# Query stage of a two-layer hybrid decoder step: query latents ahead of key latents, rope copies later, value weights split ahead of the meeting, first sample unit ahead of the first prompt unit

## The reference, cut to what matters

```python
cq = rmsnorm(cq, lw["q_norm_g"])
q = (cq @ lw["w_uq"]).reshape(B, T, MLA_HEADS, QK_NOPE + QK_ROPE)
q_pe = rope(q[..., QK_NOPE:], pos)
q_lat = jnp.einsum("bthn,chn->bthc", q[..., :QK_NOPE], lw["w_uk"])
ckv = rmsnorm(ckv, lw["kv_norm_g"])
kpe = rope(kr[:, :, None, :], pos)[:, :, 0, :]
o_lat = attend(q_lat, q_pe, ckv, kpe)
yb = jnp.einsum("bthc,chv->bthv", o_lat, lw["w_uv"]).reshape(B, T, MLA_HEADS * V_HEAD)
```

## Time and profile before

| | |
|---|---|
| median of 3 runs | 2144.66 us (2136.49 to 2145.21) |
| the profiled execution: its time / its span | 2144.24 us / 2142.4 us |
| PE busy | 2054.8 us, 96% of the span |
| PEld busy | 1898.9 us, 89% |
| DVE, ACT, POOL busy | 1199.2 us (56%), 801.8 us (37%), 402.5 us (19%) |
| matmuls | 17374 |

### The profile page before, as it was taken

One profiled execution on the slowest core, in us unless ns is written; L12 is line 12 of the kernel. 1 busy time (PEld: TensorE's weight loads), 2 busy tenths in 40 slices (PEclk: granted clock), 3 DMA queues, 4 the chain that ended last, 5 costly groups with the idle time before them and its releaser, 6 DMA issues.

```text
span 2142.4 us, 43035 instructions
## 1 busy us (share of the span) xinstructions
PE 2054.8 (96%) x17374; PEld 1898.9 (89%) x17374; DVE 1199.2 (56%) x2036; ACT 801.8 (37%) x1504; POOL 402.5 (19%) x407
## 2 busy tenths in 40 slices
PE   7989999999998999999999899999999999999997
PEld 7976667999998999999988766679999899999997
DVE  4755445333578752666757544453335886436665
ACT  4334335222354321334443333352223544213334
POOL 0025662000052000000350266610001600000012
PEclk9999999999999999999999999999999999999999
DMA  7347996222432232225451399952225232212252
GB/s 254 113 148 279 367 367 252 79 83 83 146 117 89 89 104 66 79 78 184 138 204 59 137 349 370 358 199 86 80 88 163 90 107 81 99 63 87 80 193 72
DMA packets 88849, 325.68 MB, mean 152 GB/s; under 512 B 10576, under 2 KB 15568, under 8 KB 88592
## 3 DMA queue, kind: packets, MB, share of 16 engines
q1 hardware_dynamic: 46512, 169.52, 24.2%
q0 software_dynamic: 37440, 144.98, 18.2%
q10 hardware_dynamic: 4768, 9.37, 1.3%
HBM read 315.52 MB, written 7.26 MB: 151 GB/s over the span
## 4 chain that ended last, share of the span: by engine, by line
PE 85%; DVE 9%; ACT 3%; DMA 1%; issue 1%; DVEq 1%; PEldq 0%; ACTq 0%; SPq 0%; PEld 0%
PE PS L1002 65%; PE PS L1283 6%; PE PS L1254 5%; DVE m_WL L1425 3%; PE PS L1274 2%; PE PS L1265 1%; ACT m_WH L548 1%; DVE m_X L1459 1%; DMA m_WS<-in_w_units 1%; PE PS L1306 1%; PE PS L1033 1%; PE PS L1322 1%; DVE m_XS L1470 1%; PE PS L1313 1%; PE PS L1300 1%
## 5 line engine op out<-in xcount | busy, mean ns | idle before, releaser
L1002 PE MATMUL PS<-m_XS,m_WH 128*128 128x288 f32 x5120 | 922.0, 297 | 33.8 <-DVE m_WL L1425 17.8
L1002 PEld LDWEIGHTS PS<-m_XS,m_WH 128*128 128x128 f32 x5120 | 768.0, 189 | 42.5 <-DVE m_WL L1425 20.6
L1002 PE MATMUL PS<-m_XS,m_WL 128*128 128x288 f32 x2560 | 583.5, 297 | 0.0
L1425 DVE TENSOR_TENSOR m_WL<-m_WS,m_WH 128x1024 fp32r<-128x1024 f32 (+2 forms) x284 | 369.6, 1302 | 226.8 <-ACT m_WH L548 217.9
L548 ACT ACTIVATE m_WH<-m_WS 128x1024 fp32r<-128x1024 f32 (+2 forms) x284 | 315.6, 1113 | 372.4 <-PE PS L1002 341.7
L1002 PEld LDWEIGHTS PS<-m_XS,m_WL 128*128 128x128 f32 x2560 | 423.7, 189 | 0.0
L535 POOL DMA_INDIRECT m_RAW<-in_cache_wide,m_IDXS x256 | 243.7, 952 | 398.3 <-PE PS L1002 132.9
L478 POOL TENSOR_TENSOR m_XS<-m_X 128x288 f32<-128x288 f32 x8 | 10.6, 1320 | 1169.8 <-DVE m_X L1479 1168.8
L1002 PE MATMUL PS<-m_HH,m_WH 128*128 128x288 f32 x704 | 205.6, 299 | 5.2 <-DVE m_X L1479 4.9
L1002 PE MATMUL PS<-m_HL,m_WH 128*128 128x288 f32 x704 | 203.5, 296 | 0.0
L1002 PE MATMUL PS<-m_HH,m_WL 128*128 128x288 f32 x704 | 180.3, 297 | 0.0
(11 more groups left out here) (275 smaller groups left out, 2894.1 us busy)
## 6 DMA issues: line engine op xcount, KB each, us to landing
m_WS<-in_w_units SPq DMA_DIRECT2D x232, 512.0 KB
m_WS<-in_w_units SPq DMA_DIRECT2D x48, 704.0 KB
m_RAW<-in_cache_wide,m_IDXS POOLq DMA_INDIRECT x256
m_X<-in_x_t SPq DMA_DIRECT2D x6, 576.0 KB, 7.2
m_WS<-in_w_units SPq DMA_DIRECT2D x4, 576.0 KB
x_save<-m_X POOLq DMA_DIRECT2D x4, 576.0 KB, 4.4
m_X<-x_save SPq DMA_DIRECT2D x4, 576.0 KB, 6.5
out_y<-m_X SPq DMA_DIRECT2D x8, 288.0 KB, 2.2
```

The lines of the kernel that those rows point to most:

```text
L1002: mm = pe.matmul(out(half), w(part, k), x(k)[:, half_of(half)], start=(k == 0 and part == 0 and x is xh), stop=(k == last and part == 1))
L1425: return dve.tensor_tensor(out, x, hi.bitcast(F32), ALU.subtract)
```

## The change

Nothing is computed in another way, and no engine gets another instruction but two copies that move from DVE to ACT. The lists are in another order:

- ACT and DVE split the query latents (`CQH`, `CQL`) ahead of the key-value latents (`CKS`, `CKH`, `CKL`). These now wait for the store of `o_ckv` too, since that store now stands ahead of them in ACT's list; on ACT they stand between the copies of the first and the second query tile, on DVE behind the low part of the second. `WUKH`, the split of the key weights, comes one place later.
- ACT's masked copies of the rope keys (`KPF`, `KPZ1`) stand behind the first two prompt keys.
- PE turns the second half of the rope queries between the first and second prompt keys, and DVE's `rope_query(1)` and the clearing of `OAC` change places with parts of the prompt keys.
- The split of the value weights (`WUVH` on ACT, `WUVL` on DVE) stands ahead of the meeting, and the low parts of prompt keys 2 and 3 stand behind the maxima of the sample scores.
- ACT copies half of the first sums into `OAC` (new semaphore `in_set_odd`), which were four copies on DVE.
- In unit 0, ACT and DVE serve the sample unit first and the prompt unit after it. PE's order there is as it was.

```diff
@@ ACT: ahead of the query tiles
-                act.wait_ge(S["kv_lat"], l + 1)
-                act.wait_ge(S["stored"], (l * N_STORES + 3) * 16)
-                past(act)
-                copy(CKS[:, :, :], Z[:, 3:5, SEQ:T])
-                copy(CKH[:, :, :], Z[:, 3:5, :]).then_inc(S["ck_hi"], 1)
                 act.wait_ge(S["q_lat"], l * 3 + 3)
                 for k in range(QT):
                     copy(CQH[:, k, :], Z[:, k, :]).then_inc(S["cq_hi"], 1)
...
                 query_tile(0, 0, 1)
+                act.wait_ge(S["stored"], (l * N_STORES + 4) * 16)
+                past(act)
+                copy(CKS[:, :, :], Z[:, 3:5, SEQ:T])
+                copy(CKH[:, :, :], Z[:, 3:5, :]).then_inc(S["ck_hi"], 1)
+                query_tile(1, 1, 1)
                 act.wait_ge(S["cq_lo"], (l + 1) * QT)
                 act.wait_ge(S["wuk2_in"], (l + 1) * 16)
                 copy(WUKH[:, :, :], WUK2[:, :, :]).then_inc(S["pre_hi"], 1)
-                query_tile(1, 1, 1)
...
+                act.wait_ge(S["wuv_in"], (l + 1) * 16)
+                copy(WUVH[:, :, :], WUV[:, :, :]).then_inc(S["pre_hi"], 1)
                 meet(act, "met_act", l, 0)
...
-                act.wait_ge(S["wuv_in"], (l + 1) * 16)
-                copy(WUVH[:, :, :], WUV[:, :, :]).then_inc(S["pre_hi"], 1)
                 prompt_keys(2)
                 prompt_keys(3)
...
+                act.wait_ge(S["in_pv"], l + 1)
+                for e in range(2):
+                    half = slice(64 * e, 64 * e + 64)
+                    ins = copy(OAC[half, 4 + e:7 + e:2, :], PS[half, 6, :].rearrange("p (t c) -> p t c", t=2))
+                ins.then_inc(S["in_set_odd"], 1)
...
-                        prompt_exponentials(v)
-                        exponentials(u)
+                        if u == 0:
+                            exponentials(u)
+                            prompt_exponentials(v)
+                        else:
+                            prompt_exponentials(v)
+                            exponentials(u)
@@ PE
                 prompt_keys(0)
+                turn_rope(1)
                 prompt_keys(1)
...
                 mm.then_inc(S["qs_mm"], 1)
-                turn_rope(1)
@@ DVE
-                dve.wait_ge(S["ck_hi"], l + 1)
-                lo(CKL[:, :, :], Z[:, 3:5, :], CKH[:, :, :])
                 for k in range(QT):
...
                 query_lo(1, 1)
+                dve.wait_ge(S["ck_hi"], l + 1)
+                lo(CKL[:, :, :], Z[:, 3:5, :], CKH[:, :, :]).then_inc(S["ck_lo"], 1)
...
-                    if u % 2 == 0:
-                        maxima(v)
-                        maximum(u)
+                        if u == 0:
+                            maximum(u)
+                            maxima(v)
```

More of the change, by code:

```diff
@@ L300, in build @@
                 "mask dd ya_mm ya tl sp_mm yc_bias yc",
-                "wuk_in wuv_in cq_hi cq_lo ck_hi kr_rot rot_read kpe qn_hi qr rq_mm rq_ev qpe vn_mm "
+                "wuk_in wuv_in cq_hi cq_lo ck_hi ck_lo kr_rot rot_read kpe qn_hi qr rq_mm rq_ev qpe vn_mm "
                 "qs_mm qs_even qs_odd qsp_mm",
                 "g_landed0 g_landed1 g_landed2 g_landed3 qs_turned",
-                "in_mm in_max in_exp in_turned in_pt in_pv in_set s_mm s_max s_exp p_turned "
+                "in_mm in_max in_exp in_turned in_pt in_pv in_set in_set_odd s_mm s_max s_exp p_turned "
                 "pt_ev pv_mm o_acc cmb sw_mm cdf cex dg ol_mm ols",
@@ L769, in _ @@
                     .then_inc(S["stored"], 16)
-                act.wait_ge(S["stored"], (l * N_STORES + 5) * 16)
-                past(act)
-                nc.scalar.activation(KPF[:, 0:SEQ], Z[:, 5, 0:SEQ], ACT.Copy, scale=C["rmask"][:, 0:1])
-                nc.scalar.activation(KPF[:, SEQ:T], Z[:, 5, SEQ:T], ACT.Copy, scale=C["rmask"][:, 2:3])
-                nc.scalar.activation(KPZ1[:, :], Z[:, 5, 0:SEQ], ACT.Copy, scale=C["rmask"][:, 1:2])
                 query_tile(2, 1, 2)
@@ L782, in _ @@
                 prompt_keys(1)
+                act.wait_ge(S["stored"], (l * N_STORES + 5) * 16)
+                past(act)
+                nc.scalar.activation(KPF[:, 0:SEQ], Z[:, 5, 0:SEQ], ACT.Copy, scale=C["rmask"][:, 0:1])
+                nc.scalar.activation(KPF[:, SEQ:T], Z[:, 5, SEQ:T], ACT.Copy, scale=C["rmask"][:, 2:3])
+                nc.scalar.activation(KPZ1[:, :], Z[:, 5, 0:SEQ], ACT.Copy, scale=C["rmask"][:, 1:2])
                 act.wait_ge(S["vn_mm"], l + 1)
@@ L1272, in turn_probs @@
                         pe.wait_ge(S["in_set"], l + 1)
+                        pe.wait_ge(S["in_set_odd"], l + 1)
                     for j in range(4):
@@ L1712, in _ @@
                 rope_query(0)
-                dve.wait_ge(S["ya_mm"], l * 2 + 2)
-                dve.memset(OAC[:, :, :], 0.0)
                 def prompt_keys(i):
@@ L1720, in _ @@
                 prompt_keys(0)
+                rope_query(1)
                 prompt_keys(1)
-                rope_query(1)
+                dve.wait_ge(S["ya_mm"], l * 2 + 2)
+                dve.memset(OAC[:, :, :], 0.0)
                 dve.wait_ge(S["qs_mm"], l + 1)
@@ L1727, in _ @@
                 ins.then_inc(S["qs_odd"], 1)
+                dve.wait_ge(S["vn_mm"], l + 1)
+                dve.wait_ge(S["ck_lo"], l + 1)
+                dve.wait_ge(S["stored"], (l * N_STORES + 5) * 16)
+                past(dve)
+                dve.wait_ge(S["pre_hi"], 2 * l + 2)
+                lo(WUVL[:, :, :], WUV[:, :, :], WUVH[:, :, :]).then_inc(S["pre_lo"], 1)
                 dve.wait_ge(S["qsp_mm"], l + 1)
@@ L1737, in _ @@
                 dve.memset(NMX[:, :, :], -NEG)
-                prompt_keys(2)
-                prompt_keys(3)
-                dve.wait_ge(S["pre_hi"], 2 * l + 2)
-                lo(WUVL[:, :, :], WUV[:, :, :], WUVH[:, :, :]).then_inc(S["pre_lo"], 1)
                 dve.wait_ge(S["in_mm"], l + 1)
@@ L1755, in _ @@
                     dve.tensor_copy(by_half(e, NMX)[:, e::2, 0], by_half(e, MXI)[:, :])
+                prompt_keys(2)
+                prompt_keys(3)
                 dve.wait_ge(S["in_exp"], (l + 1) * 4)
@@ L1760, in _ @@
                 dve.wait_ge(S["in_pv"], l + 1)
-                for k in range(2):
-                    for e in range(2):
-                        dve.tensor_copy(by_half(e, OAC)[:, 4 * k + e:4 * k + e + 3:2, :],
-                                        by_half(e, PS)[:, 7 - k, :].rearrange("p (t c) -> p t c", t=2))
+                for e in range(2):
+                    dve.tensor_copy(by_half(e, OAC)[:, e:e + 3:2, :],
+                                    by_half(e, PS)[:, 7, :].rearrange("p (t c) -> p t c", t=2))
                 dve.drain().then_inc(S["in_set"], 1)
@@ L1781, in accumulate @@
                     dve.wait_ge(S["o_acc"], CREDIT["o_acc"] + l * NU2 + u)
+                    if u == 0:
+                        dve.wait_ge(S["in_set_odd"], l + 1)
                     al = AL[:, b, j:j + 1]
```

## The result

The changed kernel takes 2122.51 us (median of 6 runs, 2119.47 to 2127.08) beside 2143.65 us of the kernel before (6 runs, 2136.49 to 2145.21): a ratio of 0.9911, interval [0.9896, 0.9927]. The forecast was 2124 us. The profiled execution took 2125.63 us, with a span of 2123.8.

What follows compares the result with a forecast made beforehand. PE bounds the kernel, busy for 2054.8 of 2142.4 us. Gains of 2.0 + 0.8 + 1.8 + 1.5 = 6.1 us per layer, 12.2 for two, plus clock 8.2, make 20.4 off 2144.24: 2124 us, range 2114 to 2135.

Steps and rivals of the forecast that it cites:

- Query latents first: Before the first query tile: PE's wait for `CQL` falls from 3.7 to 1.7 us, gain 2.0 us per layer.
- Second rope half: Around the prompt keys: the 1.3 us wait for `QPE` goes, 0.5 for `QSF` comes, gain 0.8 us per layer.
- Value weights: Behind the sample scores: the 2.23 us wait for `WUVL` goes, 0.4 allowed for what is late next, gain 1.8.
- Sums and sample unit first: First unit: waits for `VT8` and `AL` go, `PP` costs 0.9 to 1.1 us, gain 1.5 us per layer.
- Clock: Query stages of both layers: five stretches at the lower clock, 1.65 us each, go; gain 8.2 us.
- Sum: Whole run: 6.1 us per layer, 12.2 for two, plus clock 8.2, together 20.4 us, giving 2124 us.
- Rope copies and `WUKH`: On ACT: moving `KPF`, `KPZ1` and `WUKH` costs nothing, the rope copies bounded by about 1.5 us.
- The store: ACT waits 0.4 us for `o_ckv` between query tiles, cost 0; rival: a longer landing makes it slower, 2155, chance 0.04.
- Gathers: Attention stage: page fetches start earlier with PE, so the gain is kept; rival: gain taken back, 2139 to 2150, chance 0.08.
- The rival of a fall behind the shorter lead-in: First query tiles of one or both layers: the clock still falls behind the `CQL` wait, 2125.5 or 2127, chance 0.20.

Runs made afterwards that it cites:

- experiment 6: Changed kernel with only the clearing of `OAC` on DVE moved ahead of the first prompt key; 2121.85 us, ratio 0.9891.
- Experiment 7: Changed kernel with the prompt unit ahead of the sample unit again in unit 0, on ACT and DVE; 2126.5 us, ratio 0.9918.
- experiment 1: Changed kernel with the key-value latents split ahead of the query latents again, on ACT and DVE; 2128.07 us, ratio 0.993.
- Experiment 2: Changed kernel with value weights split behind the meeting again and low parts of prompt keys 2 and 3 ahead of the mask; 2130.56 us, ratio 0.9939.
- experiment 5: Changed kernel with PE's second rope half, DVE's `rope_query(1)` and the clearing of `OAC` all moved back; 2123.3 us, ratio 0.9895.
- run 10: The changed kernel as it was, timed and profiled a second time; 2118.03 us, ratio 0.9883 to the kernel before.
- experiment 3: Changed kernel with value weights split behind the meeting again, and nine matmuls with unused results filling PE's wait for `WUVL`; 2125.72 us, ratio 0.9921.
- experiment 4: Changed kernel with key-value latents first again, and 28 matmuls with unused results ahead of the first query tile; 2128.64 us, ratio 0.9921.

## Why the prediction was right, step by step

- **Query latents first**: forecast 2.0 us, a wait of 1.7 left. Measured 2.06, 1.66 left.
- **Second rope half**: forecast 0.8, with a new wait for `QSF` of 0.5. Measured 0.7 for the three moves together, with 0.66 of wait. The cause named, the clearing ahead of the copies, is confirmed by experiment 6.
- **Value weights**: forecast 1.8, as 2.23 less 0.4 for what is late next. Mis-sized: the part ahead of the value tiles gave 2.41, and 0.2 came back within them (8.49 against 8.28 to 8.30), so it is 2.2. What is late next costs half of what was allowed.
- **Sums and sample unit first**: forecast 1.5, with `PP` about 0.9 to 1.1 us late in two pieces. Measured 1.51, `PP` 0.73 + 0.29. Experiment 7 divides it: 0.96 by the order; the 0.55 left is by difference, and goes to the value copies.
- **Clock**: forecast five times 1.65, 8.2. All five are gone. A fall cost 1.45 to 1.68 (experiments 1, 2 and 5, and 9.86 - 8.30 = 1.56), 1.58 on the mean, some 7.9 for five. The estimate of half of a stretch of 3.4 us was a little high.
- **Sum**: 2.06 + 0.7 + 2.2 + 1.51 = 6.5 us per layer against 6.1; 12.9 + 7.9 = 20.8 against 20.4 forecast and 20.7 seen in the stages. The excess in the value weights made up for the clock. The two query stages bear the prediction out part by part. That the total came within 2 us of it (2122.51 against 2124) is partly luck, since the rest of the run moves by more than that: beside run 10 the gain was 26.2 us.
- **Rope copies and `WUKH`**: forecast nothing. No run undoes them alone, but query tiles to sample scores gave 30.34 - 28.18 = 2.16 in layer 0, and the rope moves (0.7) and one fall (1.5) use that up.
- **The store**: forecast a wait of 0.4 on ACT, hidden. Measured 0.42, with PE busy for all of 110.20 to 113.70 and no wait of PE in the second query tile.
- **Gathers**: forecast that the gain is kept. From the first value product to the mixing layer 0 takes 189.9 us (158.58 to 348.47) against 189.0 (167.58 to 356.56), with the one page wait of 0.9 in it, so 0.9 us was given back there in that execution; the second execution had 0.4 in all. The prediction put this at nothing, and that is not quite so: the kernel before shows no page waits, while ten of the twelve profiles after the change (the changed kernel and its variants) show 0.2 to 3.2 us of them.
- **The rival of a fall behind the shorter lead-in**: none in 16 stages with the wait of 1.66 us (eight executions), and none in four with 1.12. The Trainium skill, "TensorE: Matmul & The Clock Gate", section "What's actually happening", says of the rise of the clock at a kernel's start that the same kernel meets it at different counts of matmuls from run to run. By that rule nothing could be promised at the lead-in, and these runs show no fall there. Experiment 2 agrees with it for a fall: the same wait of 2.2 us brought one in one layer and not in the other.

One reason was weaker than its result. The prediction ranked waits by length, about 2 us as the edge. Length alone does not sort them: 3.7 us fell four times of four, 2.2 three of four, 2.1 (`AL`) none of four, 1.66 none of 16, but 1.29 (`QPE`) two of four. That PE's standing still brings the fall is shown for the waits of 3.7 and 2.2 us by experiments 3 and 4: with the wait filled the clock fell in none of four stages, and unfilled in seven of eight. What else decides between 1.29 and 2.1 us stays open; no run varied it. So the step that took no fall for 1.66 us came out right, but not for the reason given, since a shorter wait had falls.

## What to carry to other kernels

Where one engine is the chain, list its waits by what they wait for, shorten each by what still stands in the chain behind it, and price the next thing that becomes late: that gave 20.4 of 20.7 us here. Count the clock with the waits, since waits of 2.2 to 3.7 us at PE cost another 1.5 to 1.7 us in slow matmuls behind them in seven cases of eight; but promise it only where the wait goes altogether or is filled. And when a part is worth 1 to 3 us of 2100, read it from the boundaries of its own stage, for the total varies by more.
